# Moving tile addresses in SBUF: constants in front, and buffers at uneven distances from 8 KB

## The chip, the cores and the metric

The kernel runs on one core of a Trainium2 chip. The metric is the device time of one execution in microseconds; the median of three runs of the kernel before is 1465.08 us (1464.32 to 1465.1). On-chip data lies in SBUF, 128 partitions side by side, and every tile occupies the same byte range in each partition. An address here is the byte offset inside a partition.

## What is computed

Two layers of a hybrid decoder on 512 tokens of width 1024, all inputs in float32. The first layer mixes tokens by retention (4 heads, chunks of 128), the second by a gated DeltaNet (8 heads, chunks of 64, depthwise convolution of width 4). Each mixer and each MLP sits between two RMSNorms, and its output is added to the residual:

```
h = h + rms_norm(mixer(rms_norm(h, g0)), g1)
h = h + rms_norm(square(relu(rms_norm(h, g2) @ w_up)) @ w_down, g3)
```

The projections are the bulk of the work: 1024 to 6144 and 2048 to 1024 for retention, 1024 to 4112 and 1024 to 1024 for the DeltaNet, and 1024 to 4096 to 1024 for each MLP.

## The kernel before, in words

Every projection is done with split operands. A float32 number is split into a high part, rounded to TensorE's float32r form, and a low part, the rest. A product is then three float32r matmuls instead of one (`three` in the TensorE block): high by high, high by low, low by high. Weights come in chunks of 512 input rows by 512 columns (1 MB) into one of two buffers `w_raw`. ScalarE writes the high part (`high`, L1069) into `w_hi`, GpSimd the low part (`low_part`, L332) into `w_lo`. Activations lie as `act_hi` and `act_lo`, 8 tiles of 128 features by 512 tokens. Intermediate results of the MLP (`hid_hi`, `hid_lo`), of retention (`y_hi`, `y_lo`), of the DeltaNet (`go_hi`, `go_lo`) and up to four further weight buffers (`side_hi`, `side_lo`) share one large region, `big`, at offsets that are whole multiples of 8 KB for all of these.

A matmul has a stationary operand of 128x128, loaded by its own LDWEIGHTS (a row of 512 bytes in each partition), and a moving one of up to 512 columns (2048 bytes in each partition). In the trace the tile that moves is named first. There are these kinds:

- `act_hi,w_hi` and its two companions with 512 columns: activations move, weights are stationary (q, k and the MLP's up projections);
- `w_hi,act_hi` and companions: weights move over stationary activations (v, the retention gate, z);
- `w_hi,hid_hi`, `w_hi,y_hi`, `w_hi,go_hi` and companions: weights move over stationary data that lies in `big`;
- `act_hi,w_hi` and `act_hi,side_hi` with 256 columns: `begin`, which starts a stage while its tokens still become ready, in two halves of the tokens.

L457, L458 and L459 are the three matmuls of `part`, in the order high stationary with high moving, high stationary with low moving, low stationary with high moving. Chunks are taken four 128-row tiles (`kt`) at a time for each of four output banks (`m`). The five engines run their own instruction lists, in an order written out by hand, and wait on semaphores for each other.

All tiles are placed by class `Plan`, a counter that hands out addresses in the order of the calls. The counter starts at byte 16512. Before the change the residual comes first, then `act_hi`, `act_lo`, `w_raw`, `w_hi`, `w_lo`, each of 16 KB, and `gains`, of 8 KB. Then come three small tiles: `square` (1536 bytes, identity and masks), `dump` (2048) and `stat` (192). `big` begins behind them.

Of the kernel before, what the change touches and what calls it, by code (L numbers as in the profile page):

```python
# [7 lines left out]
F32 = mybir.dt.float32  # L8
F32R = mybir.dt.float32r
# [7 lines left out]
P = 128  # L17
D = 1024
T = 512
KT = D // P  # L20
TT = T // P
# [12 lines left out]
CK = 4  # L34
GC = 512
# [41 lines left out]
def hybrid_trunk(nc, x, norm_gains, ret_w_in, ret_gn_gain, ret_w_out, gdn_w_in, gdn_conv_w, gdn_a_log,  # L77
# [3 lines left out]
    plan = Plan(nc)  # L81
    KB = 1024

    resid = plan.tile("resid", [P, TT, D], F32)
    act_at = plan.place(32 * KB)
    act_hi = plan.tile("act_hi", [P, KT, T], F32R, act_at)
    act_lo = plan.tile("act_lo", [P, KT, T], F32R, act_at + 16 * KB)
    w_raw = plan.tile("w_raw", [P, 2, CK, GC], F32)
    w_hi = plan.tile("w_hi", [P, 2, CK, GC], F32R)
    w_lo = plan.tile("w_lo", [P, 2, CK, GC], F32R)  # L90
    gains_at = plan.place(8 * KB)
    gains = plan.tile("gains", [P, 2, D], F32, gains_at)
    square = plan.tile("square", [P, 3, P], F32)
    ident, tri, ones = (square[:, n, :] for n in range(3))
    dump_at = plan.place(2 * KB)
    dump = plan.tile("dump", [P, D], BF16, dump_at)
    stat = plan.tile("stat", [P, 12, TT], F32)
    SS_MIX, ROOT_MIX, SS_RES, ROOT_RES, NEWTON, RSTD_MIX, RSTD_RES, EPS_COL, SS_HALF, HALF_EPS = \
        0, 1, 2, 3, 4, 7, 8, 9, 10, 11
    eps = stat[:, EPS_COL, 0:1]  # L100
    big_at = plan.place(0)

    def big(name, shape, dtype, kb):
# [2044 lines left out]
```

How the kernel before makes its waits and increments, by code:

```python
            def link(self, ins):  # L253
                self.n += 1
                ins.then_inc(self.sem, 1)
                self.eng.wait_ge(self.sem, self.n)
# [14 lines left out]
            def stream(start, groups, w, chunks, col0=0):  # L271
# [4 lines left out]
                def load(g, j, cols):  # L276
                    if c0 or not isinstance(g, int):
                        sp.wait_ge(w_ready, g * (2 * chunks) + 2 * (c0 + j - 1))
                    sp.dma_start(w_raw[:, j % 2, :, :], rows[:, j * CK:(j + 1) * CK, cols])\
                        .then_inc(w_landed[j % 2], 16)
# [2 lines left out]
                    sp.dma_start(resid[:, 0, :], x[0, 0:P, :]).then_inc(sem("x_landed0"), 16)  # L284
                    sp.dma_start(gains[:, 1, :], norm_gains[0, 0, :].partition_broadcast(P))\
                        .then_inc(sem("gains_landed"), 16)
                    load(0, 0, slice(col0, col0 + GC))
                    load(0, 1, slice(col0, col0 + GC))
                    for m in (2, 3):
                        sp.dma_start(resid[:, m, :], x[0, m * P:(m + 1) * P, :]).then_inc(sem(f"x_landed{m}"), 16)
                    for j in range(2):
                        sp.dma_start(raw_side[j][:, :, :], rows[:, j * CK:(j + 1) * CK, GC:2 * GC])\
                            .then_inc(sem(f"side_landed{j}"), 16)
                    sp.wait_ge(sem("dve_low"), 1)
                with sp.Fori(0 if c0 else 2, groups) as g:
                    cols = bass.ds(sp.snap(g * GC + col0), GC)
                    for j in range(chunks):
```

## Time and profile before

| | |
|---|---|
| median of three runs | 1465.08 us |
| the profiled execution | 1464.41 us |
| its span, first to last instruction | 1462.7 us |
| TensorE busy | 1444.1 us (99%), 7772 matmuls |
| weight loads | 1214.0 us (83%), 7772 |
| VectorE, ScalarE, GpSimd busy | 575.5, 543.0 and 650.9 us |
| DMA | 136.23 MB, 93 GB/s on average |

The span is what the profiler recorded of one execution; some 1.7 us lie outside it. A matmul's busy time is not its price: matmuls are pipelined, and one with 512 columns is shown as lasting some 390 ns while the next starts after some 227 ns. What a matmul costs is the distance between two starts. From a stretch that is full of one kind it is (length of the stretch + duration of one matmul) / count, since the count of a stretch includes those that overlap its edges.

### The profile page before, as it was taken

The page shows a single profiled execution, that of the slowest core. Times are in us where ns is not written, and L with a number is a line of the kernel's source. Part 1 is how long each engine was busy: PE and PEld are TensorE (multiplying, and loading weights), DVE is VectorE, ACT ScalarE, POOL GpSimd, SP SyncE. Part 2 cuts the span into 40 slices and gives each one's busy share as a digit, 9 for nine tenths or more (in the row PEclk, how much of TensorE's full clock was granted, in tenths as well). Part 3 has the DMA queues.
Part 4 walks back from the last instruction along what each step waited for, and adds up shares of the span by engine and source line. Part 5 has one row for each costly group of instructions (what it writes and reads, how often), then busy time and mean ns, then how long its engine had stood idle before and what let it go on. Part 6 is the DMA issues. An engine that isn't in the chain of part 4 may idle for free.

```text
span 1462.7 us, 19807 instructions
## 1 busy us (share of the span) xinstructions
PE 1444.1 (99%) x7772; PEld 1214.0 (83%) x7772; DVE 575.5 (39%) x1076; ACT 543.0 (37%) x1036; POOL 650.9 (45%) x303
## 2 busy tenths in 40 slices
PE   9999999999999999999999999999999999999998
PEld 7988888757889888888888988789989988888886
DVE  5541011263254520044027344897754730024224
ACT  5232232344243222222225467764744332232231
POOL 5245344443544353444446225357445444344442
PEclk9999999999999999999999999999999999999999
DMA  6322322400233223323232222221113222322321
GB/s 244 107 87 86 113 88 87 161 12 29 90 114 116 87 86 103 99 86 109 93 116 85 92 91 85 85 85 34 58 58 131 74 99 86 107 95 86 115 87 58
DMA packets 66557, 136.23 MB, mean 93 GB/s; under 512 B 3632, under 2 KB 4016, under 8 KB 66096
## 3 DMA queue, kind: packets, MB, share of 16 engines
q1 hardware_dynamic: 64016, 125.90, 26.0%
q10 hardware_dynamic: 2464, 9.25, 1.7%
q8 instruction: 54, 0.88, 0.3%
q14 instruction: 23, 0.19, 0.0%
HBM read 133.03 MB, written 2.11 MB: 92 GB/s over the span
## 4 chain that ended last, share of the span: by engine, by line
PE 92%; POOL 2%; ACT 2%; DVE 2%; DMA 1%; issue 1%; SPq 0%; DVEq 0%; ACTq 0%
PE bank L457 28%; PE bank L458 27%; PE bank L459 27%; PE bank L672 2%; POOL side_lo L332 1%; PE bank L658 1%; PE bank L788 1%; PE bank L744 1%; POOL w_lo L332 1%; PE bank L510 1%; DMA w_raw<-in_ret_w_in_dram 1%; DVE gq L1905 1%; DVE resid L1673 1%; PE bank L690 0%; PE bank L992 0%
## 5 line engine op out<-in xcount | busy, mean ns | idle before, releaser
L332 POOL TENSOR_TENSOR w_lo<-w_raw,w_hi 128x1024 fp32r<-128x1024 f32 (+1 forms) x216 | 516.6, 2414 | 672.1 <-ACT w_hi L1069 657.8
L1069 ACT ACTIVATE w_hi<-w_raw 128x1024 fp32r<-128x1024 f32 x206 | 207.0, 1055 | 470.5 <-PE bank L459 427.9
L457 PE MATMUL bank<-act_hi,w_hi 128*128 128x512 f32 (+1 forms) x816 | 293.2, 359 | 1.0 <-DVE act_lo L1713 0.6
L459 PE MATMUL bank<-act_hi,w_lo 128*128 128x512 f32 (+1 forms) x816 | 292.1, 358 | 0.0
L458 PE MATMUL bank<-act_lo,w_hi 128*128 128x512 f32 (+1 forms) x816 | 292.1, 358 | 0.0
L458 PE MATMUL bank<-w_lo,hid_hi 128*128 128x512 f32 x480 | 189.0, 394 | 0.0
L457 PE MATMUL bank<-w_hi,hid_hi 128*128 128x512 f32 x480 | 188.2, 392 | 0.0
L459 PE MATMUL bank<-w_hi,hid_lo 128*128 128x512 f32 x480 | 186.4, 388 | 0.0
L1827 DVE TENSOR_TENSOR relu_sq<-relu 128x512 f32<-128x512 f32 x64 | 48.5, 758 | 328.6 <-ACT relu L1101 328.0
L457 PEld LDWEIGHTS bank<-act_hi,w_hi 128*128 128x128 f32 x816 | 153.9, 189 | 23.8 <-DVE act_lo L1713 1.1
L459 PEld LDWEIGHTS bank<-act_hi,w_lo 128*128 128x128 f32 x816 | 153.9, 189 | 22.8
L458 PEld LDWEIGHTS bank<-act_lo,w_hi 128*128 128x128 f32 x816 | 153.9, 189 | 22.1
L457 PE MATMUL bank<-w_hi,act_hi 128*128 128x512 f32 x320 | 125.0, 391 | 0.3 <-POOL w_lo L332 0.3
L459 PE MATMUL bank<-w_hi,act_lo 128*128 128x512 f32 x320 | 124.5, 389 | 0.0
L458 PE MATMUL bank<-w_lo,act_hi 128*128 128x512 f32 x320 | 124.5, 389 | 0.0
L457 PEld LDWEIGHTS bank<-w_hi,hid_hi 128*128 128x128 f32 x480 | 90.1, 188 | 20.9
L459 PEld LDWEIGHTS bank<-w_hi,hid_lo 128*128 128x128 f32 x480 | 90.1, 188 | 20.2
L458 PEld LDWEIGHTS bank<-w_lo,hid_hi 128*128 128x128 f32 x480 | 90.2, 188 | 18.0
L457 PE MATMUL bank<-act_hi,side_hi 128*128 128x256 f32 x256 | 72.3, 282 | 1.4 <-POOL side_lo L332 1.4
L1776 DVE TENSOR_TENSOR gate<-gate,gains x16 | 13.0, 816 | 153.6 <-ACT gate L1101 153.6
L1101 ACT ACTIVATE relu<-bank 128x512 f32<-128x512 f32 x64 | 38.0, 597 | 91.2 <-PE bank L459 91.2
L457 PEld LDWEIGHTS bank<-w_hi,act_hi 128*128 128x128 f32 x320 | 60.1, 188 | 13.5 <-POOL w_lo L332 1.2
(285 smaller groups left out, 2146.3 us busy)
## 6 DMA issues: line engine op xcount, KB each, us to landing
w_raw<-in_mlp_w_up_dram SPq DMA_DIRECT2D x32, 1024.0 KB, 5.8
w_raw<-in_mlp_w_down_dram SPq DMA_DIRECT2D x32, 1024.0 KB, 5.0
w_raw<-in_ret_w_in_dram SPq DMA_DIRECT2D x22, 1024.0 KB, 5.1
w_raw<-in_gdn_w_in_dram SPq DMA_DIRECT2D x16, 1024.0 KB, 5.4
w_raw<-in_ret_w_out_dram SPq DMA_DIRECT2D x8, 1024.0 KB, 5.0
w_raw<-in_gdn_w_out_dram SPq DMA_DIRECT2D x4, 1024.0 KB, 4.9
gains<-in_norm_gains_dram ACTq DMA_DIRECT2D x7, 512.0 KB, 4.7
raw_side<-in_ret_w_in_dram SPq DMA_DIRECT2D x2, 1024.0 KB, 15.0
```

The lines of the kernel that those rows point to most:

```text
L332: done = nc.gpsimd.tensor_tensor(LO[slot][:, kt, :], RAW[raw][:, kt, :], HI[slot][:, kt, :].bitcast(F32), ALU.subtract)
L457: pe.matmul(dst, sta_hi, mov_hi, start=first, stop=False)
L458: pe.matmul(dst, sta_hi, mov_lo, start=False, stop=False)
L459: return pe.matmul(dst, sta_lo, mov_hi, start=False, stop=last)
L510: done = pe.transpose(turned(m, k), normed[:, m % 2, k * P:(k + 1) * P], ident)
L658: done = pe.matmul(bank[i][:, 0:T - i * P], qk_t[:, KT + 2 * h + d, i * P:(i + 1) * P], qk_t[:, 2 * h + d, i * P:T], start=d == 0, stop=d ...
L672: done = pe.matmul(bank[4 + j][:, :], score[:, h % 2, i, j * P:(j + 1) * P], v_tm[:, i, h * RV:(h + 1) * RV], start=i == 0, stop=i == j)
L744: last = pe.transpose(bank[b][:, n * P:(n + 1) * P], src[:, h, n * P:(n + 1) * P], ident)
L788: done = pe.matmul(bank[b][:, n * P:(n + 1) * P], gk[:, h, n * P:(n + 1) * P], other[:, h, n * P:(n + 1) * P], start=True, stop=True)
L1069: act.activation(HI[raw if slot is None else slot][:, kt, :], RAW[raw][:, kt, :], ACT.Copy)\
L1101: act.activation(dst, bank[4 * p + m][:, :], func).then_inc(emptied, 1)
L1827: dve.tensor_tensor(relu_sq[:, m, :], relu[:, m, :], relu[:, m, :], ALU.mult)\
```

## The change

Only addresses change; no instruction is added, removed or reordered. The three small tiles go in front of the residual, the residual is put on a multiple of 512 bytes, and gaps of 64, 64, 128 and 256 bytes are put in. `act_at + ...` tiles that share the activation region keep their offsets, except `act_lo`.

```diff
-    resid = plan.tile("resid", [P, TT, D], F32)
-    act_at = plan.place(32 * KB)
-    act_hi = plan.tile("act_hi", [P, KT, T], F32R, act_at)
-    act_lo = plan.tile("act_lo", [P, KT, T], F32R, act_at + 16 * KB)
-    w_raw = plan.tile("w_raw", [P, 2, CK, GC], F32)
-    w_hi = plan.tile("w_hi", [P, 2, CK, GC], F32R)
-    w_lo = plan.tile("w_lo", [P, 2, CK, GC], F32R)
-    gains_at = plan.place(8 * KB)
-    gains = plan.tile("gains", [P, 2, D], F32, gains_at)
     square = plan.tile("square", [P, 3, P], F32)
     ident, tri, ones = (square[:, n, :] for n in range(3))
     dump_at = plan.place(2 * KB)
     dump = plan.tile("dump", [P, D], BF16, dump_at)
     stat = plan.tile("stat", [P, 12, TT], F32)
+    plan.at = (plan.at + 511) // 512 * 512
+    resid = plan.tile("resid", [P, TT, D], F32)
+    act_at = plan.place(32 * KB + 64)
+    act_hi = plan.tile("act_hi", [P, KT, T], F32R, act_at)
+    act_lo = plan.tile("act_lo", [P, KT, T], F32R, act_at + 16 * KB + 64)
+    w_raw = plan.tile("w_raw", [P, 2, CK, GC], F32)
+    plan.at += 64
+    w_hi = plan.tile("w_hi", [P, 2, CK, GC], F32R)
+    plan.at += 128
+    w_lo = plan.tile("w_lo", [P, 2, CK, GC], F32R)
+    gains_at = plan.place(8 * KB)
+    gains = plan.tile("gains", [P, 2, D], F32, gains_at)
...
+    plan.at += 256
     big_at = plan.place(0)
```

The addresses that result, as remainders by 8192 counted from the residual's address:

| tile | before | after |
|---|---|---|
| resid, act_hi | 0 | 0 |
| act_lo | 0 | 64 |
| w_raw | 0 | 64 |
| w_hi | 0 | 128 |
| w_lo | 0 | 256 |
| gains | 0 | 256 |
| big (hid, y, go, side) | 3776 | 512 |

The residual itself moves from 16512 to 20480.

## Rows read from the trace of the kernel before

**Rows 1.** The page's busy line and its line of the granted TensorE clock:

```profile
PE 1444.1 (99%) x7772; PEld 1214.0 (83%) x7772; DVE 575.5 (39%) x1076; ACT 543.0 (37%) x1036; POOL 650.9 (45%) x303
...
PEclk9999999999999999999999999999999999999999
```

**Rows 2.** The page's chain that ended last, by engine:

```profile
PE 92%; POOL 2%; ACT 2%; DVE 2%; DMA 1%; issue 1%; SPq 0%; DVEq 0%; ACTq 0%
```

**Rows 3.** Waits of TensorE, longest in total: line, releaser, us, times, longest:

```profile
PE bank L510 <- DVE normed L1691: 3.6, 3, 1.3
```

**Rows 4.** TensorE's groups with shapes apart: count, busy us, mean ns:

```profile
L457 PE MATMUL bank<-act_hi,w_hi 128*128 128x512 f32 x576 | 225.0, 391 | 0.0
...
L457 PE MATMUL bank<-w_hi,hid_hi 128*128 128x512 f32 x480 | 188.2, 392 | 0.0
...
L457 PE MATMUL bank<-w_hi,act_hi 128*128 128x512 f32 x320 | 125.0, 391 | 0.3 <-POOL w_lo L332 0.3
...
L457 PE MATMUL bank<-act_hi,side_hi 128*128 128x256 f32 x256 | 72.3, 282 | 1.4 <-POOL side_lo L332 1.4
...
L457 PE MATMUL bank<-act_hi,w_hi 128*128 128x256 f32 x240 | 68.2, 284 | 1.0 <-DVE act_lo L1713 0.6 <-POOL w_lo L365 0.3
...
L457 PE MATMUL bank<-w_hi,y_hi 128*128 128x512 f32 x112 | 44.4, 397 | 0.0
...
L457 PE MATMUL bank<-w_hi,go_hi 128*128 128x512 f32 x64 | 25.4, 397 | 0.0
...
L457 PE MATMUL bank<-side_hi,hid_hi 128*128 128x512 f32 x32 | 12.6, 394 | 0.0
...
L457 PE MATMUL bank<-side_hi,y_hi 128*128 128x512 f32 x16 | 6.4, 397 | 0.0
```

**Rows 5.** TensorE in stretches of one kind: length, busy (count), clock, DMA:

```profile
107.00:280.00 173.00, 173.00 (x765) 1.00 0.30 101
520.00:607.00 87.00, 87.00 (x382) 1.00 0.29 94
609.00:694.00 85.00, 85.00 (x376) 1.00 0.28 93
...
695.00:760.00 65.00, 65.00 (x286) 1.00 0.29 94
430.00:440.00 10.00, 10.00 (x86) 1.00 0.59 202
...
52.00:63.00 11.00, 11.00 (x96) 1.00 0.55 176
466.00:476.00 10.00, 10.00 (x90) 1.00 0.31 105
```

**Rows 6.** All engines in two equal stretches: PE, PEld, DVE, ACT, POOL, clock, DMA:

```profile
191.00:206.00 15.00, 15.00 (x68) 12.43 (x67) 0.00 (x0) 4.32 (x6) 4.84 (x3) 1.00 0.37 130
206.00:221.00 15.00, 15.00 (x68) 12.43 (x67) 4.37 (x4) 6.36 (x8) 8.45 (x4) 1.00 0.21 70
```

**Rows 7.** Timeline from 12.8 us, to 13.6 and to 14.2: bf16 warm-up matmuls:

```profile
12.81 1.03 PE L582 MATMUL bank<-warm 128*128 128x512 bf16 x4
...
12.81 1.46 PE L582 MATMUL bank<-warm 128*128 128x512 bf16 x6
```

**Rows 8.** The chain by time: float32 transposes of 128 columns:

```profile
326.43 1.75 PE bank L690 x16
```

**Rows 9.** Timeline, TensorE: first and tenth 512-column matmul after the 256-column ones:

```profile
63.03 0.40 PE L457 MATMUL bank<-act_hi,w_hi 128*128 128x512 f32 x1
...
65.12 0.39 PE L457 MATMUL bank<-act_hi,w_hi 128*128 128x512 f32 x1
```

**Rows 10.** Line 332 on GpSimd: durations in ns, least, median, greatest:

```profile
L332 POOL TENSOR_TENSOR w_lo<-w_raw,w_hi x216: 1284/2409/2870, 13.1 to 1426.4; 128x1024 fp32r<-128x1024 f32 x100, 128x512 fp32r<-128x512 f32 x8
L332 POOL TENSOR_TENSOR side_lo<-w_raw,side_hi x18: 2426/2442/3454, 400.6 to 1431.2; 128x1024 fp32r<-128x1024 f32 x18
```

**Rows 11.** Line 1069 on ScalarE, the same columns:

```profile
L1069 ACT ACTIVATE w_hi<-w_raw x206: 1038/1052/1215, 14.9 to 1423.9; 128x1024 fp32r<-128x1024 f32 x103
L1069 ACT ACTIVATE side_hi<-w_raw x18: 1039/1042/1068, 396.6 to 1425.8; 128x1024 fp32r<-128x1024 f32 x18
```

**Rows 12.** The chain by time, at the start: the wait for the first weights:

```profile
1.75 9.22 DMA w_raw<-in_ret_w_in_dram
```

## The prediction

> **What bounds the kernel now.** I read the page's busy line and clock first, then the chain, the waits of TensorE, its groups by shape, and last the stretches that hold one kind of matmul. TensorE is busy 1444 of 1463 us at the full 2.4 GHz (the clock row is in tenths, and 9 is 90% or more; the stretches of rows 5 say 1.00) [rows 1, 5]. The chain that ends last is 92% TensorE [rows 2], and the longest of its waits in total is 3.6 us [rows 3]. So only the distance from one matmul's start to the next can move the time by more than a few us. The change touches no instruction, so it can act only through that distance, through the duration of other engines' instructions, or through DMA.
>
> The distance, by (stretch + one duration) / count [rows 5], durations 0.39 us with 512 columns and 0.28 us with 256 [rows 4]:
>
> - weights moving over stationary activations, 107 to 280 us: 173.39 / 765 = 226.7 ns; activations moving over weights, 609 to 694 us: 85.39 / 376 = 227.1 ns. One matmul more or less in the count is 0.6 ns here and 0.3 in the first, so these are one value, 226.7.
> - weights moving over hid, 520 to 607 us: 87.39 / 382 = 228.8 ns; 695 to 760 us: 65.39 / 286 = 228.6 ns. I take 228.7.
> - 256 columns of activations over w_hi and w_lo, 430 to 440 us: 10.28 / 86 = 119.5 ns.
> - 256 columns of activations over side_hi and side_lo: 52 to 63 us 11.28 / 96 = 117.5 ns, and 466 to 476 us 10.28 / 90 = 114.2 ns.
>
> What would these be without any disturbance? The bf16 warm-up matmuls with 512 columns, each with its own weight load, follow each other by (1.46 - 1.03) / 2 = 215 ns [rows 7]. Sixteen float32 transposes of 128 columns take 1.75 / 16 = 109.4 ns each [rows 8]; they take as many array cycles as a float32r matmul with 256 columns would, if I read 109.4 against half of 215. So a float32r matmul with 512 columns pays about 12 to 14 ns above the undisturbed distance, one with 256 columns 5 to 10. That is some 4800 times 12 ns, 58 us, and this is all that the change can win on TensorE.
>
> Does it come from outside or from inside TensorE? In 191 to 206 us GpSimd is busy 4.84 us and VectorE not at all; in 206 to 221 us they are busy 8.45 and 4.37 us; DMA goes from 0.37 to 0.21. The count of matmuls is 68 in both [rows 6]. So it doesn't depend on what other engines do. What is left is the pair that TensorE itself reads at one time: the moving operand, and the weights that are loaded for the next matmul. And it does depend on where these two lie: with 256 columns, the same instruction with the same moving tile costs 119.5 ns where the stationary tile is w, a multiple of 8 KB away, and 117.5 or 114.2 where it is side, 3776 bytes off such a multiple. With 512 columns it goes the other way: 226.7 at a distance of 0, 228.7 at 3776. The stationary slices step by 512 bytes from bank to bank and the distance stays the same through all four, so what counts is the remainder by 512 or less: 0 against 192.
>
> The Trainium skill speaks against the whole change. "SBUF — State Buffer", section "Who interferes with whom", gives TensorE two independent SBUF read ports and has it never wait on anyone, and names no bank in SBUF. By it every tile address is worth the same and the sum is zero; that is a rival below. The rows above agree with it as to the other engines, and don't as to TensorE's own pair, 119.5 against 114.2 ns.
>
> **The change part by part.** All distances by 512 change. Stationary minus moving, before and after: activations with w (either way round) 0, then 128 for high with high and 192 for low with low; big with moving w 192, then 384 and 256; side with moving activations 192, then 0 or 448. The trace of before holds only two remainders, 0 and 192, so the new ones have no row of their own. I bound them by the nearest.
>
> 1. Weights over hid, y and go: 3 x (480 + 112 + 64) = 1968 matmuls [rows 4]. They stand now at the worse of the two seen values. New remainders 384 and 256, both even multiples of 128, as 0 is and 192 isn't. I take the value of 0: 1968 x (228.7 - 226.7) = 3.9 us less. Bounds: 215 ns, 27.0 us less; and 232.2 ns, 6.9 us more. The upper end is the mean distance of nine matmuls just behind a change of kind, before the pattern has settled: (65.12 - 63.03) / 9 [rows 9].
> 2. Activations with w, 512 columns, 3 x (576 + 320) = 2688, and side over hid and y, 3 x (32 + 16) = 144: 2832 [rows 4]. They stand at the better seen value. Of the three matmuls of a product two get a remainder of 128 and one gets 192. I take no change. Bounds: 215 ns, 33.1 us less; 232.2 ns, 15.6 us more. With the 228.7 ns that the remainder of 192 shows it is 5.7 us more.
> 3. 256 columns over w: 3 x 240 = 720 [rows 4], 119.5 to 117.5 ns: 1.4 us less. Bounds: 109.4 ns, 7.3 us less; nothing more, since no stretch shows a worse mean.
> 4. 256 columns over side: 3 x 256 = 768 [rows 4]. Those at 114.2 ns are two stages, some 190 matmuls; I let them lose that and stand at 117.5: 0.6 us more. Bounds: 109.4 ns for all, some 5.5 us less; 119.5 ns for all, 2.6 us more.
> 5. GpSimd's low parts, whose three tiles lie at a distance of 0 now: median 2409 ns (a few are half as long), and 2442 ns with side, at 3776 [rows 10]. ScalarE's high parts: 1052 and 1042 ns [rows 11]. No effect within 1.5%, and both wait for TensorE most of the time. Zero. If the cover were gone: GpSimd is on the chain for 2%, 29 us [rows 2], and 1.5% of that is 0.4 us, either way.
> 6. DMA into w_raw now begins at 64 past a multiple of 128 bytes instead of on one. Only the first load is on the path, 9.22 us [rows 12]; later ones are issued far ahead. Were it 10% slower, that is 0.9 us. Taken as zero, bound 1 us either way.
> 7. The constants in front cost nothing by themselves: the transposes read `square` either way and show no disturbance [rows 8]. Everything else in float32 at half the column rate (scores, attention, the DeltaNet) is taken as unchanged: zero, bound 1 us.
>
> Sum against the profiled execution: 1464.4 - 3.9 - 1.4 + 0.6 = 1459.7 us. The median of the runs is 0.7 above that execution, so 1460.
>
> **The rivals.**
>
> *The settled pattern of the activation kinds is lost (slower).* At a distance of 0 all three matmuls of a product have the same distance, which may be why they settle at 226.7. With 128 and 192 mixed in one product it settles at 228.7 as over hid, or not at all. The place is the 2832 matmuls of term 2, the price 5.7 us at 228.7 and 15.6 at 232.2. It decides from 1.7 ns per matmul on, where it eats up the 4.7 us won. With term 1 at nothing, 3 and 4 as above: 1464.4 + 5.7 - 0.8 + 0.7 = 1470 us; with 232.2 ns for both, 1464.4 + 15.6 + 6.9 - 0.8 + 0.7 = 1487. For it: every remainder other than 0 that the trace shows with 512 columns is worse than 0. Against: there is only one such remainder, and with 256 columns the same one is better.
>
> *The distances really part the two reads (much faster).* The 256-column stages at 114.2 ns pay some 5 ns instead of 10. If the 4800 matmuls with 512 columns came to 5 ns above 215, so 220: 2832 x 6.7 + 1968 x 8.7 = 36.1 us less, 1429 us with 3 and 4. If they came half that way, 1447. For it: two different costs for the same instructions at the same addresses (117.5 and 114.2) show that lower patterns exist. Against: no 512-column stretch shows one.
>
> *The change does nothing that can be measured.* Only the remainder by some smaller unit counts and gains and losses cancel, or the rule of the two ports holds and the differences seen come from the operand kinds. 1465 us. Against: 119.5 and 117.5 with the same instruction.
>
> **How the numbers follow.** Forecast (small gain, mostly over hid, y and go) 0.32; pattern lost, 1470 to 1487, 0.34; parted in earnest, 1429 to 1447, 0.19; nothing, 1465, 0.15. What a measurement of this kernel can tell from no change is about 0.2%, 2.9 us. Of the forecast some 0.28 lies beyond it, and with 0.19 that is 0.47 faster. Within 0.2%: 0.15, a little of the forecast and of the slower case, less what "nothing" may hide, 0.18. Slower 0.35. The range that holds it 8 times in 10 goes from 1430 to 1480; the forecast's own is 1454 to 1463.
>
> **What would show it.** The same stretches give each term: the stage over hid at 226.7 ns would show term 1; the 765 matmuls of the v and gate stage in 173 us (226.7 ns) show whether the activations' pattern holds; the half-width stages at 117.5 show terms 3 and 4. GpSimd's 2409 and ScalarE's 1052 ns should stand. If the forecast is wrong, it will be because the untested remainders 128, 256 and 384 cost something that the two seen ones don't tell, above all in term 2, which has most of the matmuls.

## The result, and the profile after

The changed kernel takes 1479.41 us (median of 4 runs, 1479.23 to 1479.62) against 1465.04 us of the kernel before in the same runs: 1.010 times the time, 95% interval 1.0087 to 1.0112. That is 14.4 us slower. The forecast was 1460 us, 5 us faster; the measured time lies outside its own 1454 to 1463 us and just inside the wide range of 1430 to 1480.

The profiled execution has a span of 1477.5 us, 14.8 more than before. The page's busy line:

```profile
PE 1459.0 (99%) x7772; PEld 1215.3 (82%) x7772; DVE 576.7 (39%) x1076; ACT 542.9 (37%) x1036; POOL 655.6 (44%) x303
```

TensorE's busy time grows by 14.9 us with the same 7772 matmuls; VectorE and ScalarE stand, GpSimd gains 4.7 us beside the path. The longest of TensorE's waits is 3.9 us in total (3.6 before [rows 3]), so the loss isn't one wait but lies in the distance between matmuls:

```profile
PE bank L514 <- DVE normed L1695: 3.9, 4, 1.3
```

The stretches of one kind, in the columns of rows 5 (stretch, length, busy, count, clock, DMA):

```profile
107.00:280.00 173.00, 173.00 (x757) 1.00 0.30 99
520.00:607.00 87.00, 87.00 (x382) 1.00 0.29 97
610.00:695.00 85.00, 85.00 (x366) 1.00 0.31 99
...
52.00:63.00 11.00, 11.00 (x94) 1.00 0.53 169
470.00:480.00 10.00, 10.00 (x86) 1.00 0.33 105
```

By (stretch + one duration) / count: weights moving over activations 173.39 / 757 = 229.0 ns (226.7 before); activations moving over weights 85.39 / 366 = 233.3 (227.1 before, from a count of 376); weights over hid 87.39 / 382 = 228.8, unchanged to the matmul; half-width over side 10.28 / 86 = 119.5 where it was 114.2 [rows 5]. DMA and clock are as before: a share of 0.29 to 0.31 in the long stretches and a clock of 1.00.

Adding up, over all matmuls of a kind, the time from each start to the next matmul's start gives where the time went:

| kind, columns | matmuls | before, us | after, us |
|---|---|---|---|
| activations over w, 512 | 1728 | 394.9 | 405.4 |
| w over activations, 512 | 960 | 219.0 | 221.1 |
| w over hid, y, go, 512 | 1968 | 452.8 | 452.7 |
| activations over side, 256 | 768 | 92.3 | 94.5 |
| activations over w, 256 | 768 | 95.8 | 96.0 |

The differences sum to 14.9 us, the whole of the span's 14.8. ("Weights over activations" are weights that move over stationary activations.)

The groups by shape show the same for the kind that suffers most. Its mean is a modelled duration, and so only a sign, but the high by high one of them has grown from 391 to 394 ns [rows 4], and the other two, 389 ns before, to 395 and 397:

```profile
L462 PE MATMUL bank<-act_lo,w_hi 128*128 128x512 f32 x576 | 228.8, 397 | 0.0
L463 PE MATMUL bank<-act_hi,w_lo 128*128 128x512 f32 x576 | 227.4, 395 | 0.0
L461 PE MATMUL bank<-act_hi,w_hi 128*128 128x512 f32 x576 | 227.2, 394 | 0.0
```

The other engines' instructions didn't move. GpSimd's low parts have a median of 2427 ns (2409 before) [rows 10], the first load takes 9.11 us (9.22 before) [rows 12]:

```profile
L336 POOL TENSOR_TENSOR w_lo<-w_raw,w_hi x216: 1296/2427/2898, 13.0 to 1441.3; 128x1024 fp32r<-128x1024 f32 x100, 128x512 fp32r<-128x512 f32 x8
```

```profile
1.74 9.11 DMA w_raw<-in_ret_w_in_dram
```

### The profile page after: what moved, and what is told of

Read it like the earlier page. It is cut to its first block, busy times and chain, and to the rows that moved or that the text cites. A ratio compares the mean times of both kernels' runs of the same rounds, so it can differ in the third digit from the quotient of the medians.

```text
span 1477.5 us, 19807 instructions
## 1 busy us (share of the span) xinstructions
PE 1459.0 (99%) x7772; PEld 1215.3 (82%) x7772; DVE 576.7 (39%) x1076; ACT 542.9 (37%) x1036; POOL 655.6 (44%) x303
## 4 chain that ended last, share of the span: by engine, by line
PE 92%; POOL 2%; ACT 2%; DVE 2%; DMA 1%; issue 1%; SPq 0%; DVEq 0%; ACTq 0%
PE bank L461 28%; PE bank L463 28%; PE bank L462 27%; PE bank L676 2%; POOL side_lo L336 1%; PE bank L662 1%; PE bank L748 1%; PE bank L792 1%; POOL w_lo L336 1%; PE bank L514 1%; DMA w_raw<-in_ret_w_in_dram 1%; DVE gq L1909 1%; DVE resid L1677 1%; PE bank L694 0%; PE bank L996 0%
## 5 line engine op out<-in xcount | busy, mean ns | idle before, releaser
L462 PE MATMUL bank<-act_lo,w_hi 128*128 128x512 f32 (+1 forms) x816 | 296.1, 363 | 0.0
L463 PE MATMUL bank<-act_hi,w_lo 128*128 128x512 f32 (+1 forms) x816 | 295.4, 362 | 0.0
L462 PE MATMUL bank<-act_lo,side_hi 128*128 128x256 f32 x256 | 72.3, 283 | 0.0
```

Of the source, the lines that this page charges most:

```text
L462: pe.matmul(dst, sta_hi, mov_lo, start=False, stop=False)
L463: return pe.matmul(dst, sta_lo, mov_hi, start=False, stop=last)
```

## The experiments

There are two kinds. Some are the full kernel with another layout. The others leave all of the layers out: the output is a copy of x, and TensorE runs streams of matmuls on a tile of ones, each line of the program one stream, all other engines idle. Each such program ran once. Written out, a stream is

```
for n in range(36):   # a pair at a distance of d bytes
    pe.matmul(bank[n // 12 % 7], fill[:, (16384 + d) // 4:][:, 0:128], fill[:, 0:512],
              start=n % 12 == 0, stop=n % 12 == 11)
```

with the output first, then the stationary operand, then the moving one. A distance is the stationary operand's address less the moving one's. The cost is read from the chain by time: (length of the stream) / (number of matmuls). A stream "settles" when its starts repeat one pattern; the settled value is the mean from start to start over its last two thirds.

### Streams at chosen distances

> Leaves out the whole layer work: TensorE runs long streams of float32r matmuls, each with its own weight load, at chosen distances in bytes between stationary and moving operand; the output is a copy of x. Theory A (the distance by 512 sets a settled cost): streams at one distance settle; distance 0 gives 226.7 ns per matmul with 512 columns, 3776 (192 by 512) 228.9, and 512, 1024, 2048 and 4096 give the value of 0; moving both operands together by 64 to 192 changes nothing; the triples reproduce the full kernel: 226.7 (act,w before), 233.3 (act,w after), 229 (w,act after), 228.9 (w,hid both). Rival B (another engine or DMA takes part in the full kernel): with nothing else running, all streams stand at 215 to 216 ns. Rival C (only absolute addresses count, the start of each operand by 128 or 256): moving both by 64 changes the value by 2 ns or more, and the distance alone does not.

The chain by time, columns start, us, line, count. L66 to L82 are distances 0, 64, 128, 192, 256, 320, 384, 448 and 512:

```profile
36.34 8.21 PE bank L66 x36
44.55 8.40 PE bank L68 x36
52.95 8.37 PE bank L70 x36
61.31 8.25 PE bank L72 x36
69.56 8.18 PE bank L74 x36
77.74 8.40 PE bank L76 x36
86.14 8.37 PE bank L78 x36
94.51 8.25 PE bank L80 x36
102.75 8.18 PE bank L82 x36
110.94 8.16 PE bank L84 x36
```

The series repeats from L74 on: what counts is the distance by 256 bytes. Settled, the values are 226.7 ns at 0, 233.3 at 64, 232.1 at 128 and 228.9 at 192; 1024 (L84) gives 8.16 / 36 = 226.7. So the remainder of 128 isn't like 0, as term 1 had assumed, but the second worst of these four. Moving both operands together by 64, 128 or 192 gave 226.7, 233.3 and 228.9 again for distances of 0, 64 and 192: rival C, absolute addresses, falls for these pairs. Rival B falls too: all of this happens with nothing else running.

With 256 columns the order is another, and 0 is the dearest: 120.0 ns at 0, 117.8 at 64 and 192, 118.6 at 128.

The kernel's own groups of three matmuls, with the addresses of before and after (L132 activations over w before, L134 after, L136 w over activations after, L138 and L140 w over hid before and after):

```profile
300.36 24.55 PE bank L132 x108
324.91 24.96 PE bank L134 x108
349.87 24.73 PE bank L136 x108
374.61 24.74 PE bank L138 x108
399.34 24.73 PE bank L140 x108
```

L136 gives 229.0 ns, L138 229.1 and L140 229.0: the kernels' 229.0, 228.7 and 228.8. Hid went from three distances of 192 to a mix of 128 and 0 and got the same price. L134 gives 231.1 ns and not the 233.3 of the full kernel, so for this kind the stream has only two thirds of the loss.

### The constants in front, without the gaps

Against the changed kernel, lines in between left out; the comments are added here, also in the diffs below:

```diff
-    act_at = plan.place(32 * KB + 64)
+    act_at = plan.place(32 * KB)
-    act_lo = plan.tile("act_lo", [P, KT, T], F32R, act_at + 16 * KB + 64)
+    act_lo = plan.tile("act_lo", [P, KT, T], F32R, act_at + 16 * KB)
-    plan.at += 64          # in front of w_hi
-    plan.at += 128         # in front of w_lo
-    plan.at += 256         # in front of big
+    plan.at += 512
```

> Only the constants go in front and big lies a multiple of 512 from the weights; activations, low part and both weight buffers stay multiples of 8 KB apart. Theory A: activation kinds with 512 columns stay at 226.7 ns, hid at 226.7 instead of 228.9 if only the remainder by 512 counts: 1960 to 1465 us. Read as 1460 to 1465 us. Rival C (absolute addresses): 1470 us or more, since every tile of the change's front part has moved by 3968 bytes.

Every large tile now lies at the same remainder by 256, big at 512 by 8192. Measured: 1462.25 us against 1464.8, ratio 0.9983, 95% interval 0.9974 to 0.9993. The stretches 110 to 280, 612 to 695 and 521 to 606 us:

```profile
110.00:280.00 170.00, 170.00 (x752) 1.00 0.31 102
612.00:695.00 83.00, 83.00 (x368) 1.00 0.31 101
521.00:606.00 85.00, 85.00 (x377) 1.00 0.28 91
```

170.39 / 752 = 226.6, 83.39 / 368 = 226.6 and over hid 85.39 / 377 = 226.5 ns. Start to start, the 1968 matmuls over hid, y and go take 448.5 us where they took 452.8, 4.3 less, and the half-width ones over side 94.8 instead of 92.3, 2.5 more; the span is 2.2 us shorter. So these rows show no cost of the constants in front, and placing big where the other tiles are is a gain over hid, y and go and a smaller loss over side.

### The gaps, without the constants in front

Against the kernel before:

```diff
-    act_at = plan.place(32 * KB)
+    act_at = plan.place(32 * KB + 64)
-    act_lo = plan.tile("act_lo", [P, KT, T], F32R, act_at + 16 * KB)
+    act_lo = plan.tile("act_lo", [P, KT, T], F32R, act_at + 16 * KB + 64)
+    plan.at += 64          # in front of w_hi
+    plan.at += 128         # in front of w_lo
```

> Only the gaps of 64, 64 and 128 bytes at the activations' low part and the two weight buffers; constants stay behind. Theory A: the activation kinds cost what they cost after the change, 233.3 ns (activations moving) and 229 ns (weights moving), so 1476 to 1481 us. Rival C: 1465 us within 3, since residual and high part of the activations have not moved.

Measured: 1480.3 us against 1464.8, ratio 1.013, interval 1.0092 to 1.0168 (four runs, three within 0.4 us and one at 1490.99 us, which makes the interval wide). The gaps alone cost as much as the whole change. Stretches 110 to 280, 612 to 695 and 521 to 606 us:

```profile
110.00:280.00 170.00, 170.00 (x745) 1.00 0.30 99
612.00:695.00 83.00, 83.00 (x361) 1.00 0.31 100
521.00:606.00 85.00, 85.00 (x369) 1.00 0.30 99
```

w over activations 228.7, activations over w 231.0, over hid 231.4 ns. The middle one was expected at 233.3: the same addresses relative to each other as in the changed kernel, and a cost between that kernel's and 226.7. Over all 1728 of them it is 231.9 ns, which makes 8.3 us more than before where the changed kernel has 10.5, and the matmuls over hid, y and go, which aren't at the changed kernel's distances here (64 and 192 in place of 128 and 0), add 4.1 us. The total came out as expected for partly another reason.

The mean of 231.9 hides two values. The stages with activations moving that follow half-width matmuls (from 64, 481, 850 and 1161 us) run at 233.3 ns, most others, the two long ones that follow a stage over hid (from 615 and 1294 us) among them, at 231.1. These are the same instructions on the same buffers in one execution. Two matmuls 155 starts apart in a stage of the first sort, and two 157 starts apart in one of the second:

```profile
69.76 0.39 PE L459 MATMUL bank<-act_hi,w_hi 128*128 128x512 f32 x1
105.93 0.40 PE L461 MATMUL bank<-act_hi,w_lo 128*128 128x512 f32 x1
...
639.63 0.39 PE L461 MATMUL bank<-act_hi,w_lo 128*128 128x512 f32 x1
675.92 0.40 PE L459 MATMUL bank<-act_hi,w_hi 128*128 128x512 f32 x1
```

36.17 / 155 = 233.4 ns and 36.29 / 157 = 231.1. So this group of three can settle at either value at one set of addresses; in the changed kernel all of these stages but a short last one stand at 233.3.

### Everything 64 apart

Against the kernel before:

```diff
+    plan.at += 64          # in front of w_raw
+    plan.at += 128         # in front of big
```

> The full kernel of before with two gaps: 64 bytes in front of the raw weights and 128 in front of big, so that w lies 64 behind the activations and big 64 behind w. Theory A with the values of the single pairs (stationary minus moving 64: 233.3 ns, 192: 228.9): activations moving 1728 x 6.7 ns, weights over activations 960 x 2.2, weights over hid, y and go 1968 x 4.6, half-width stages about -1: 1464.8 + 11.5 + 2.1 + 9.0 - 1 = 1486 us. Rival C (absolute addresses): within 3 us of 1465, since all tiles stay on multiples of 64.

This layout was worked out from the single pairs before it ran. Measured: 1484.88 us against 1465.12, ratio 1.0136, interval 1.0119 to 1.0153; expected 1486. Stretches 110 to 280, 612 to 695 and 521 to 606 us:

```profile
110.00:280.00 170.00, 170.00 (x745) 1.00 0.30 99
612.00:695.00 83.00, 83.00 (x357) 1.00 0.31 100
521.00:606.00 85.00, 85.00 (x366) 1.00 0.30 99
```

With weights moving the distance is 192: 170.39 / 745 = 228.7 ns. With activations moving, and over hid, it is 64: 83.39 / 357 = 233.6 and 85.39 / 366 = 233.3 ns. Where all matmuls of a group have one distance, the values of the pairs foretell the full kernel: 21.6 us more by their sum, 19.8 measured.

### Distances in steps of 8 bytes

> Leaves out the layer work, as the streams before; one pair per stream, distance in steps of 8 bytes from 0 to 248, with 512 columns, and of 16 bytes with 256. Theory A (collisions of two readers that step through 256 bytes of banks): the cost is periodic in 256 bytes, 226.7 ns at 0 and 233.3 at 64 as seen, and between multiples of 64 it lies within 224 to 236, with no distance that comes to 216. Rival D (a distance that parts the readers altogether exists, but off the multiples of 32): some stream at 216 to 220 ns.

L66 and L70 are distances 0 and 16, L94 is 112, L96 120, L120 216:

```profile
35.56 8.21 PE bank L66 x36
...
52.08 8.40 PE bank L70 x36
...
152.74 8.40 PE bank L94 x36
161.14 8.17 PE bank L96 x36
...
261.31 8.17 PE bank L120 x36
```

Of 38 distances (every 8 bytes and six between) none is below 8.17 / 36 = 226.9 ns. Besides 0 only 120 and 216 reach 226.7 settled; 20 of the others stand at 233.3, one (96) at 234.3, the other 14 between 228.3 and 232.3. Rival D falls: no distance tried comes near 216 ns. Activations and w had 0 in the layout of before and so were already at the least that a pair of 512 columns reached. And 192 gave 233.3 here, where the first streams gave 228.9.

### Narrower, shorter and other types

> Leaves out the layer work; streams at distances 0, 64, 128 and 192 with narrower stationary operands, shorter moving ones, plain float32 and bf16. Theory A: what a matmul pays above 215.8 ns is paid while the next weights are read, so it falls with the stationary width (128 columns some 11 ns at distance 0, 64 columns about half, 32 about a quarter) and hardly with the moving length; plain float32 (429 ns, half the column rate) and bf16 (216 ns, half the bytes) pay nothing at any distance. Rival E (float32r matmuls have a fixed cost of their own, the distance only modulates it): narrow stationary operands still pay 8 ns or more.

L68 is a stationary operand of 32 columns, L76 one of 64, L92 of 128, all at a distance of 0. L132 and L138 are 448 moving columns at distances 0 and 192:

```profile
35.39 8.34 PE bank L68 x36
...
68.71 8.27 PE bank L76 x36
...
135.09 8.17 PE bank L92 x36
...
242.69 7.31 PE bank L132 x36
...
264.62 7.20 PE bank L138 x36
```

The three widths settle at 231.7, 230.0 and 226.7 ns, 96 columns at 230.0. A quarter of the weights doesn't lower the price, so theory A's second half, that the price is paid while the weights are read, falls; rival E holds: with 512 columns every float32r stream pays 11 ns or more beside bf16's 215.8, and the distance only changes how much more. With 384 moving columns it is 173.3 ns, with 512 226.7: the slope between them is (226.7 - 173.3) / 128 = 0.417 ns per column, one per cycle at 2.4 GHz, and the fixed part 13.3 ns. With 448 columns that part is 13.3 ns at a distance of 192 (200.0 ns) and 16.0 at 0 (202.7 ns), so 0 is not the best distance for every length. Plain float32 and bf16 with 512 columns (L142 is float32 at 64, L154 bf16 at 192) show no effect of the distance at 0, 64, 128 and 192, 429 and 215.8 ns:

```profile
282.12 10.30 PE bank L142 x24
...
336.33 7.77 PE bank L154 x36
```

### History, and which pair it is

> Leaves out the layer work. First four streams alternate two matmuls so that either a matmul's own operands lie 0 apart and its moving operand 64, 128 or 192 from the next stationary one, or the other way round. Theory F (what collides is the moving operand with the weights loaded for the next matmul): own 64 and 192 with next 0 gives 226.7 ns, own 0 with next 64 and 192 gives 228.9 or more. Rival G (own pair counts): the reverse. Then pairs at 0, 64 and 192 and the triple of the changed kernel, each behind 1, 2, 4, 7 or 11 half-width matmuls. Theory H (a stream settles in one of a few repeated patterns, chosen by the moment at which it starts): distance 0 always 226.7, distance 192 in some streams 228.9 and in others 233.3, the triple in some 231.1 and in others 233.3. Rival I (the 233.3 of the full kernel comes from its stepping through 2048 and 512 byte slices): all triples 231.1, only the last but one stream 233.3.

Both F and G fall. With a matmul's own operands at 0 and the next weights at 64 and 192 a stream of 60 takes 13.90 us (L66), the other way round 13.89 (L68), both settled at 231.6; with 128 it is 228.3 (L70) and 230.0 (L72). Neither pair alone is the one that counts.

History: distance 0 came to 226.7 all five times, 64 to 233.3 all five times, 192 four times to 228.9 and once to 233.3. L96 is one of the four, L120 is the other one, behind seven half-width matmuls:

```profile
138.52 9.17 PE bank L96 x40
...
197.60 9.33 PE bank L120 x40
```

Between two starts, the four repeat patterns around 226, 229, 232 ns, and the one stays at 233 and 234. The same instructions at the same addresses can thus settle in two ways, by what ran before them; that it is the moment at which the stream begins, as theory H has it, isn't shown. The group of three of the changed kernel didn't: 13.87 us for 60, 231.2 ns, all five times, and 231.1 with the kernel's own steps of 2048 and 512 bytes. Rival I falls. That this group too has a second value, 233.3 ns, is shown by the stages of the kernel with the gaps alone; what picks it stays open, since half-width matmuls in front didn't do it here.

### Only the low part of the activations apart

Against the kernel before:

```diff
-    act_at = plan.place(32 * KB)
+    act_at = plan.place(32 * KB + 64)
-    act_lo = plan.tile("act_lo", [P, KT, T], F32R, act_at + 16 * KB)
+    act_lo = plan.tile("act_lo", [P, KT, T], F32R, act_at + 16 * KB + 64)
+    plan.at += 192         # in front of w_raw
+    plan.at += 64          # in front of big
```

> The full kernel with all tiles at the same remainder by 256 bytes, except the low part of the activations, 64 behind. Only one weight load in three of the activation kinds sees a distance other than 0. Theory by the mean of single pairs: activations moving 227.4 ns (1728 x 0.7 = 1.3 us), weights moving over activations 228.9 (960 x 2.2 = 2.1 us), hid at 226.7: 1462.3 + 3.4 = 1465.7 us. Rival H (one odd load tips the whole pattern): both kinds at 229 to 233.3, 1462.3 + 6 to 18 = 1468 to 1480 us.

Measured: 1472.54 us against 1465.17, ratio 1.0052, interval 1.0035 to 1.0068, and 10.2 us over the layout with all remainders equal. Start to start, activations over w cost 232.0 ns, w over activations 231.1. One 64-byte gap at one of the four tiles adds 5.3 and 4.4 ns to 226.7 on the average of a group, where the mean of its three pairs has 0.7 and 2.2. That mean (1465.7 us in all) is no guide for mixed groups.

### Mixed streams, and the best layout again

> Leaves out the layer work; streams in which only the stationary or only the moving operand changes its address from matmul to matmul, all else at distance 0. Theory J (every odd remainder in a repeated group of matmuls costs, whichever operand carries it, and the whole group settles at 1.7 to 6.7 ns above 226.7): all streams with a 64, 128 or 192 at 228 ns or more, also those with one odd member in three, and the last stream, whose addresses differ only by multiples of 256, at 226.7. Theory by the mean of single pairs: one odd stationary operand in three costs two thirds of nothing and one third of the pair's surplus, 227.4 to 228.9 ns. Rival K (an odd moving operand costs nothing by itself, since what counts is where the weights lie): streams with the stationary operand fixed at 226.7.

L76 is a fixed stationary operand with moving ones at 0 and 192, L78 one stationary operand in three at 64, L90 the low part of the activations alone with activations moving, L92 the same with w moving, L94 addresses that differ by multiples of 256:

```profile
118.88 16.33 PE bank L76 x72
135.20 22.18 PE bank L78 x96
...
268.22 22.28 PE bank L90 x96
290.50 22.18 PE bank L92 x96
312.67 21.77 PE bank L94 x96
```

L94 gives 226.8 ns. All others stand at 228.9 ns or more, except L76, which settles at 226.7; so theory J holds but for one stream of fourteen, and rival K falls (a fixed stationary operand with moving ones at 0 and 64 costs 16.62 / 72 = 230.8). L90 and L92, 232.1 and 231.0 ns, are the full kernel's 232.0 and 231.1 of the experiment before.

> The layout with all large tiles at one remainder by 256 bytes and the constants in front, timed once more with more rounds. Theory J: 1462.3 us again, 2.6 us or 0.18% below the kernel before, with an interval that leaves out 1; the stages over hid, y and go give all of it (1968 x 2.2 ns = 4.4 us less), the half-width stages over side give 2 to 3 us back. Rival (the first timing was chance): within 0.05% of before.

Measured: 1462.38 us (11 runs) against 1465.08 (15 runs), ratio 0.9983, interval 0.9974 to 0.9992. The layout with all large tiles at one remainder by 256 beats both kernels, by 0.18% and 1.2%.

## Why the prediction was wrong

**What held.** The time from one matmul's start to the next was the only thing that moved the time (14.9 us of 14.8), other engines and DMA have no part in it, and the price hangs on the distances between TensorE's own operands by some small power of two, 256 in the streams, where moving both operands together changed nothing. Terms 5 to 7 were zero as said: 2427 and 1050 ns on the two engines, 9.11 us for the first load.

**Term 2 is the step that failed.** It took no change for the matmuls between activations and w, with 5.7 us for the rival. Measured: 10.5 us more with activations moving and 2.1 with weights moving, 12.6 together, near the rival's upper price of 15.6. The step had two faults. It took a distance of 128 to cost what 0 costs; as a pair it costs 232.1 ns. And it had the distances wrong: two of 128 and one of 192, "for low with low", a product that `three` never makes. By the table of addresses the three matmuls have 128, 64 and 256 with activations moving, so one stands at 64, the dearest of the four at 233.3 ns, and 128, 0 and 192 by 256 with weights moving. Mixed in a group they cost 233.3 and 228.9 ns in nearly all stages. The layout of before had these at 0, the least that was seen with 512 columns. The 144 matmuls of side over hid and y, also in term 2, kept their distance of 0 to each other and cost 0.1 us more.

**Term 1 failed by the same assumption**, that even multiples of 128 are like 0. It had 3.9 us less; measured 0.1 less. The gain itself was real: when big was put at a remainder of 0 by 256 the three kinds over it gave back 4.3 us. The step mistook which layout does that.

**Terms 3 and 4.** Half-width over w had 1.4 us less, on 720 of the 768 matmuls (48 stand under another line), and came out at 0.2 more; half-width over side had 0.6 more and came out at 2.2 more, since none of its stages kept the 113 to 114 ns. By its own rows term 4's upper bound was 2.2 us, not 2.6 (578 x 2.0 ns and 190 x 5.3), and the time went all the way there.

**The picture behind them** was wrong in one more way. The prediction read the 12 to 14 ns above bf16 as a disturbance, and 58 us as what a change could win. The streams showed at least 10.9 ns over bf16 with 512 columns at every distance tried, a fixed part of 13.3 ns over the columns' own time. Over big only 4.3 us were to be had, 2.7 us net, and the rival of much faster had no ground. What it took as its sign, 117.5 and 114.2 ns "at the same addresses", isn't one: the stages from 52 and 1138 us use the side buffers of slots 4 and 5 in `HEAD_SLOTS`, those from 466 and 829 us slots 3 and 4, 8 KB off. Whether that or what ran before sets them apart isn't shown.

**The rivals.** "The settled pattern of the activation kinds is lost" was right in its place and its sign, and the changed kernel lies in its span of 1470 to 1487 us. Its mechanism was right in that the mixed distances give up the 226.7; but the stages with activations moving do settle, at 233.3 ns, above the 232.2 that it took as the most, and those with weights moving at 228.9. It had 0.34 and the forecast 0.32. The trace of before had one sign for it, that the only other remainder seen with 512 columns was the worse one, and the forecast gave term 1 the benefit of the same sign without a row for 128. The case of no effect was not borne out either. One of its two grounds is in the Trainium skill, "SBUF — State Buffer", section "Who interferes with whom", by which the ports for TensorE's moving operand and for its weight loads are independent. For float32r the measured 14.4 us, from addresses alone, speak against it; for plain float32 and bf16 every stream agrees with it.

## What to carry to other kernels

Where split float32r matmuls with 512 moving columns fill TensorE, put all moving and stationary tiles at one remainder by 256 bytes; with 256 columns and with 448 another distance was cheaper (117.8 against 120.0 ns, 200.0 against 202.7), and the layout with one remainder paid 2.5 us for that; constants of odd size go where they don't shift the large tiles against each other. An uneven gap isn't a way to part two readers unless the price of that very distance has been measured, and a stream of 36 matmuls measures it in 8 us of chip time, though one stream shows only one of the values in which a distance can settle. Where a group of matmuls repeats with mixed distances, measure the group: the mean of its pairs is off by as much as the effect (1465.7 us against 1472.54).

## What the runs showed that was not expected

- Settled streams repeat short patterns. The most frequent means are 34 and 35 times 6.67 ns (226.7 and 233.3), half-width ones 17 and 18 times (113.3 and 120.0); 228.9 (a pattern of 226, 229, 232) lies a third of the way between the first two. 6.67 ns are 16 cycles at 2.4 GHz. No run shows what keeps such a period.
- Weight loads of 32 columns made a float32r matmul slower (231.7 ns) and not faster than those of 128 (226.7), at a distance of 0.
- With 128 and with 192 moving columns a float32r matmul costs the same 111.7 ns.
- 192 bytes gave 228.9 or 233.3 ns by what ran before, and the group of three at the changed kernel's distances 231.1 or 233.3 ns in one execution at the same addresses.
- In the kernel with everything 64 apart the half-width matmuls over w took 93.5 us where they took 95.8 before, about half of them at 113.3 ns.
